# One 64x64 inverse product of the RWKV-7 scan, issued in slot 10 of the group before instead of slot 0 of its own

## The reference

```
def _wkv7_step(S, inp):
    r_t, w_t, k_t, v_t, aa_t, bb_t = inp
    sa = jnp.einsum('zbhij,zbhj->zbhi', S, aa_t)
    S = S * w_t[..., None, :] + sa[..., :, None] * bb_t[..., None, :] + v_t[..., :, None] * k_t[..., None, :]
    y = jnp.einsum('zbhij,zbhj->zbhi', S, r_t)
    return S, y
...
    seq = tuple(jnp.moveaxis(_flip_bwd(z), 2, 0) for z in (r2, w_h, k_h, v2, aa, bb))
    _, ys = lax.scan(_wkv7_step, S0, seq)
```

## Time and profile before

| | |
|---|---|
| median of three runs | 4420.51 us (4414.08 to 4432.33) |
| the profiled execution | 4417.87 us |
| its span, first to last instruction | 4415.9 us |
| mean granted TensorE clock | 0.970 |
| PE busy | 4071.9 us (92%) |
| DVE / ACT / POOL busy | 2155.6 / 1389.2 / 1301.5 us |
| line 1710 (P), PE | 296.3 us in x6400 records |
| lines 1721 and the last level's 1723 | 228.0 us in x5120, and x1280 |

### The profile page before, as it was taken

How to read it: one execution, slowest core, us unless ns; L and a number is a source line. 1 busy time by engine, 2 the same in 40 slices (tenths; PEclk the granted TensorE clock), 3 DMA queues, 4 the chain that set the end, 5 groups by cost and what they waited for, 6 DMA issues and landing times. The chain is left out here.

```text
span 4415.9 us, 108166 instructions
## 1 busy us (share of the span) xinstructions
PE 4071.9 (92%) x47874; PEld 3463.4 (78%) x47874; DVE 2155.6 (49%) x3514; ACT 1389.2 (31%) x2961; POOL 1301.5 (29%) x901
## 2 busy tenths in 40 slices
PE   5999899999999998899958888888879999999999
PEld 5889567888888887788757777777757888888888
DVE  5662462352352442446657777777743343252441
ACT  3331572211111112234435555555532211111111
POOL 3111233211111112122146556566534211111111
PEclk8999899999999998999979999999989999999999
DMA  4222333212213113122232222222143212313213
GB/s 126 71 80 73 121 104 108 68 37 88 81 38 122 51 45 108 63 77 72 96 101 79 80 69 82 69 80 82 46 166 101 81 39 74 98 39 99 69 37 109
DMA packets 354145, 356.39 MB, mean 81 GB/s; under 512 B 18640, under 2 KB 325072, under 8 KB 351632
## 3 DMA queue, kind: packets, MB, share of 16 engines
q1 hardware_dynamic: 352096, 345.19, 24.5%
q10 hardware_dynamic: 1584, 4.27, 0.3%
HBM read 247.16 MB, written 102.24 MB: 79 GB/s over the span
## 5 line engine op out<-in xcount | busy, mean ns | idle before, releaser
L442 POOL TENSOR_TENSOR mo_wlow<-mo_raw,mo_whigh 128x1024 fp32r<-128x1024 f32 (+1 forms) x148 | 350.5, 2368 | 1671.2 <-ACT mo_whigh L529 1671.2
L509 PE MATMUL f_ps<-fx_hh,mo_whigh 128*128 128x512 f32 (+1 forms) x2112 | 529.8, 359 | 0.0
L509 PE MATMUL f_ps<-fx_hl,mo_whigh 128*128 128x512 f32 (+1 forms) x2112 | 529.0, 358 | 0.0
L509 PE MATMUL f_ps<-fx_hh,mo_wlow 128*128 128x512 f32 (+1 forms) x2112 | 528.8, 358 | 0.0
L529 ACT ACTIVATE mo_whigh<-mo_raw 128x1024 fp32r<-128x1024 f32 (+1 forms) x148 | 152.3, 1029 | 863.7 <-PE f_ps L509 863.7
L509 PEld LDWEIGHTS f_ps<-fx_hl,mo_whigh 128*128 128x128 f32 x2112 | 349.1, 189 | 65.4
L509 PEld LDWEIGHTS f_ps<-fx_hh,mo_wlow 128*128 128x128 f32 x2112 | 349.1, 189 | 65.4
L509 PEld LDWEIGHTS f_ps<-fx_hh,mo_whigh 128*128 128x128 f32 x2112 | 349.2, 189 | 64.9
L594 DVE TENSOR_TENSOR f_xo<-f_ps,f_xo 128x512 f32<-128x512 f32 x168 | 90.8, 596 | 611.9 <-PE f_ps L509 579.9
L509 PE MATMUL f_ps<-mo_oh,mo_whigh 128*128 128x512 f32 (+1 forms) x1440 | 362.9, 360 | 9.9 <-PEq L56 9.9
L509 PE MATMUL f_ps<-mo_ol,mo_whigh 128*128 128x512 f32 (+1 forms) x1440 | 360.6, 359 | 0.0
(11 more groups left out here) (293 smaller groups left out, 8449.5 us busy)
## 6 DMA issues: line engine op xcount, KB each, us to landing
f_xo<-xres SPq DMA_DIRECT2D x64, 640.0 KB, 4.0
xres<-f_xo SPq DMA_DIRECT2D x48, 640.0 KB, 2.9
mo_raw<-in_ffn_w_gate SPq DMA_DIRECT2D x44, 512.0 KB, 3.8
mo_raw<-in_ffn_w_up SPq DMA_DIRECT2D x44, 512.0 KB, 3.7
sc_rk<-rkvl SPq DMA_DIRECT2D x80, 256.0 KB, 3.2
rkvl<-ri_ot SPq DMA_DIRECT2D x28, 640.0 KB
mo_raw<-in_ffn_w_down SPq DMA_DIRECT2D x32, 448.0 KB, 4.5
qkv_raw<-in_na_w_qkv SPq DMA_DIRECT2D x24, 512.0 KB, 5.5
```

The costliest lines, as they stand in the source:

```text
L442: nc.gpsimd.tensor_tensor(wlow[:, m % 2, 0:kt], raw[:, 0:kt], whigh[:, m % 2, 0:kt].bitcast(F32), ALU.subtract).then_inc(cut_lo, 1)
L509: last = nc.tensor.matmul(ps[:, m % 2, n, 0:count], w[:, m % 2, k], x[:, k, t0:t0 + count], start=(k == 0 and w is whigh and x is xh), sto ...
```

## The change

`inverse(G, n)` no longer issues anything in slot 0. In slot 10, where P of level INV would be due, it takes P of level 0 of the next group (Gp = G + 1) and interleaves it with T of z = 1, level 4, of group G, two matmuls of the one and two of the other for each chunk. `p_copy` on ACT follows: its copy moves from slot 0 to slot 10, into the place behind `u_copy` and ahead of `fade_state`. What is computed is unchanged, and so is the number of instructions; DVE, POOL and SP keep their order.

```diff
                 def inverse(G, n):
-                    if not group(G) or n > 2 * INV:
+                    if n == 0 or n > 2 * INV:
                         return
                     k, odd = divmod(n, 2)
                     zp = 1 if odd else 0
                     kt = k if odd else k - 1
-                    does_p, does_t = k < INV, kt >= 0
+                    Gp = G
+                    if k == INV:
+                        Gp, k = G + 1, 0
+                    does_p, does_t = group(Gp), group(G)
                     if does_t:
                         level_t_waits(G, 1 - zp, kt)
                     if does_p:
-                        level_p_waits(G, zp, k)
+                        level_p_waits(Gp, zp, k)
                     for s in range(U):
                         for h in range(2):
                             if does_p:
-                                last_p = level_p(G, zp, k, s, h)
+                                last_p = level_p(Gp, zp, k, s, h)
...
                 def p_copy(G, n):
+                    if n == 0 or n > 2 * INV:
+                        return
                     k, z = divmod(n, 2)
-                    if not group(G) or k >= INV:
+                    if k == INV:
+                        G, k = G + 1, 0
+                    if not group(G):
                         return
                     act.wait_ge(pe_p[z], 5 * G + k + 1)
```

## The result

The changed kernel takes 4438.18 us (median of 5 runs, 4436.96 to 4443.01), the kernel before 4420.51 (4414.08 to 4432.33): a ratio of 1.0044, 95% interval 1.0032 to 1.0055. It is 17.7 us slower, less than the 22 us that were set as the bound for slower, and inside the range of 4408 to 4446. The forecast of 4428 had the sign, and half of the size: it was worked out as 8.7 us.

What follows compares the result with a forecast made beforehand. No engine alone was the bound; who waits for whom was, with gram and POOL pinned to DVE's slot 11. 38 x 0.23 = 8.7 us on 4417.87 gave 4426.6, or 4429.2 beside the median; forecast 4428, range 4408 to 4446.

Steps and rivals of the forecast that it cites:

- P is not free in slot 10: Slot 10 on PE: P and T share two quadrants, so both take 0.93 us, 0.46 more than T alone.
- Nothing is to be had from slot 0: Slot 0: removing P frees 0.46 us of PE, but gram waits for DVE's queries, with 0.13 to 0.21 us slack.
- The rival in which the saving arrives: Slots 10 and 0: P and T run side by side or gram's waits don't hold; up to 17.5 us less, 4403; chance 0.08.
- T's result is late at DVE, and with it queries and gram: Slots 10 to 0: DVE takes T 0.27 us after S starts; gram comes 0.14 or 0.32 us later by group.
- The sign to look for: Slot 0 on PE: gram stands behind an idle gap, released by DVE's line 2010, where there was none.
- X is released by ACT's second copy of turn: Slot 11: turn's copies end at 2867.95, so X starts about 2868.0, later after DVE's state than the 0.05 of now.
- The size: 0.23 a group, 8.7 us: Per group: mean of 0.14 and 0.32 us later gram, over 38 groups, 8.7 us slower.
- the rival of P held by DVE: Slot 10: P waits for DVE's slot 9 update and holds T; 0.35 us shift gives 22 us, 4442; chance 0.17.
- The copy of P ahead of the fades: ACT, slot 10: P's copy delays the fades, making DVE's state product wait no more than 0.05 us.
- The half and half of the two kinds of group: Half the groups have gram 0.14 us later, half 0.32; all of one kind gives 5.3 us, of the other 12.2.
- Back to back on one quadrant: Slot 10 rival: successive matmuls on one quadrant don't overlap, 0.22 us a record; 67 us slower, 4487; chance 0.03.
- No change: Scan rival: PE waits without a releaser end at fixed times and swallow a 0.2 us lateness; 4420; chance 0.22.

Runs made afterwards that it cites:

- The other quadrants: Changed kernel with P of slot 10 written to the other PSUM half, so P and T use four quadrants: 1.0047; with ACT's copy also behind the turn copies: 1.0013.
- the kernel with the bare gap: Changed kernel with ACT's copy of P in slot 10 moved behind the two turn copies, PE unchanged: 4442.48 us, ratio 1.0035.
- the two kernels in which T goes first: Changed kernel with slot 10 issuing T whole, then P: 1.0011 with ACT's copy of P behind the turn copies, 1.0060 with it ahead of the fades.
- the kernel with 3200 more instructions: Kernel before with 20 extra 64x64 matmuls per group in slot 10 on free quadrants, result read by nobody: 4468.73 us, ratio 1.0092.

## Why the prediction was right, and where its size was off

*P is not free in slot 10.* Right: 0.93 from the first of P and T to S, as predicted, with lines 1710 and 1723 alternating. The other quadrants give 0.54.

*Nothing is to be had from slot 0.* Right but for a little, and shown by itself: P cut away there gives 0.9997, at most 5.3 us of 15.6. The rival in which the saving arrives falls with it.

*T's result is late at DVE, and with it queries and gram.* Right: the gap of DVE ahead of its slot 10 update is there (31.1 us in 49 waits, 13.6 in 22 before). Predicted 0.27 after S, measured 0.22 in the group shown. The gap of PE ahead of gram that was to show it is not in the changed kernel: X came so late by ACT that its matmuls reach to gram. It is there as soon as ACT's copy is out of the way. The wait was real all the same: gram starts 0.06 behind the queries in the median, and 0.32 behind X, where it follows after 0.28 in the groups in which X itself is late (2.4 and more after S). In the kernel with the bare gap the 0.06 is the same and the 0.32 is 0.60. The forecast of gram at S + 2.29 (2868.32 - 2866.03) stands against a median of 2.33. The sign to look for was badly chosen.

*X is released by ACT's second copy of turn.* Right as to the releaser. That the time came out to the hundredth in the group shown is luck: forecast at about S + 1.97 (2868.0 against S at 2866.03), measured 2950.22 - 2948.25 = 1.97, with a median of 2.01. The copies were forecast to end at S + 1.92 and X to follow at once; they end at S + 1.71 (2949.96 - 2948.25), and X starts 0.26 behind them, in this group and in most. The prediction had no term for the time from ACT's end to PE's start, and it had ACT's block too late by about as much.

*The size: 0.23 a group, 8.7 us.* This is the term that was mis-sized; 17.7 us is 0.47 a group. By the profiles:

```
                                       predicted   measured (two pairs)
slot 10, from P beside T                  +0.46    +0.64  +0.58
slots 11 and 0, given back                -0.23    -0.15  -0.20
slots 1 to 9                               0       +0.10  +0.10
group                                     +0.23    +0.59  +0.48
```

- Slot 10 is 0.12 to 0.18 above the charge of P. In means over 38 groups the first inverse product of slot 10 starts 1.33 after U, against 1.23 before (1.32 and 1.25 in the later pair), and from it to S it is 1.07 against 0.54 (1.06 and 0.55): 0.53 and 0.51 more, not 0.46, the excess being gaps without a releaser. The later start is mostly the rival of P held by DVE: in 6 groups of the one profile and 8 of the other P starts 0.21 or 0.22 behind the end of DVE's slot 9 update, some 0.34 later than usual, which makes 0.05 to 0.07 a group. In the clearest of these

```profile
2797.97 0.28 DVE L2100 TENSOR_TENSOR sc_rf<-sc_inv_ps,sc_rf 128x128 f32<-128x128 f32 x1
```
```profile
2798.01 0.28 PE L1692 MATMUL sc_gram_ps<-sc_small,sc_vb 64*64 64x64 f32 x4
2798.47 0.33 PE L1710 MATMUL sc_inv_ps<-sc_tf,sc_bl 64*64 64x64 f32 x4 [0.18 <-issue]
...
2799.34 0.27 PE L1723 MATMUL sc_inv_ps<-sc_rf,sc_pt_last 64*64 64x64 f32 x1 [0.41 <-issue]
```

  DVE's update of slot 9 ends at 2798.25 and P starts 0.22 later, though the profile writes "issue" in front of it: a wait that was put down to nobody. That it is this wait shows in the two kernels in which T goes first: there, as in the kernel before, the first product of slot 10, which is T's, starts up to 0.13 and 0.21 ahead of the end of that update in such groups, and none is held. The same slot has a second gap, 0.41 in the middle of T, in which no semaphore is waited for. The rival was right in kind, in 6 to 8 of 38 groups and not in all.
- The copy of P ahead of the fades. The prediction gave it "no more than 0.05 of wait". In 31 of 36 groups, the one shown among them, state starts 0.13 after the fades' end, neither more nor less, and 0.85 to 0.89 after DVE took T, where in the kernel before that is 0.81. So the fades do set the start of state in nearly every group, by some 0.05: what was said. Here too two things cancelled, fades that end at S + 0.95 in the group shown and not at S + 1.12 (2867.15 - 2866.03), and 0.13 from ACT's end to DVE's start that the prediction left out. What was wrong was to price the copy alone. Put behind turn's copies it gives back little in the changed order (1.0044 and 1.0038 against 1.0035), but 1.0047 - 1.0013 = 15 us with free quadrants, of which the profiles show 8, and 21.7 us with T first. The prediction counted ACT's copy as a small addition to DVE's lateness; it is a second wait of about the same length beside it.
- The half and half of the two kinds of group was right: 19 groups of the kernel before have gram 0.12 or 0.13 behind the queries, 14 have it 0.18 to 0.22 behind. In medians slots 11 and 0 give back what was forecast: S to the next U is 3.28 before and 3.05 after.
- With the two pairs of profiles as far apart as they are, the split of the 0.24 (0.47 less 0.23) among these is not settled. What is shown is that the copy behind turn's copies, together with either free quadrants or T ahead of P, leaves 5 or 6 us of the loss (1.0011 and 1.0013).

*Back to back on one quadrant.* The rival with 67 us is out: 32 records on two quadrants take 0.93, 58 ns for each on its quadrant.

*No change.* The rival said that fixed gaps would swallow a lateness of 0.2. They did not: the gaps without a releaser are as long as before (118.3 and 123.0 us after, 115.4 and 123.3 before, from 2300 to 3220 us), and the loss came on top.

*What stays open.* The last 5 us in the kernels without both waits: 8 extra matmuls a group on free quadrants also cost 4.9 us, but P is not extra, it is moved, so that the number of instructions is the same. That both are 5 us need not be one cause. A change of order or of number also moves the instructions against the 16,384-byte packets of the next section but one, and no run moves them alone.

## What to carry to other kernels

Before you move work out of a slot, cut it away there and time that: here the answer, 0.9997, would have said that the best outcome is about no change. When a product is put beside another one, count three things apart: the part of the array that both use, the semaphores that the second one waits for on behalf of the first, and the copy that follows it on the next engine, with all that stands behind that copy. And when two such waits are about equally long, each edit alone looks worthless; try them in pairs before you drop either.

## What the runs showed of the hardware

The gaps of PE that nothing releases are not spread at random. In 37 groups of the kernel before, the trace has 219 packets of 16,384 bytes on the queue of kind "instruction", 5.92 for a group, and the 119 such gaps of over 0.15 us (115.4 us) end 1.39 us after the landing of one of them in the median (80% between 1.25 and 1.51, all between 1.20 and 1.64; with a packet every 4 us, gaps at chance times would fall into so narrow a band one time in nine). In the kernel with 3200 more instructions all 139 gaps end 1.20 to 1.64 us after a landing too. Not every packet has a gap. Its row over 2300 to 3220 us (packets, MB, share of 16 DMA engines):

```profile
q8 instruction: 229, 3.75, 1.6%
```

There are 58,457 records of PE in 40 groups, 247 for a packet, so that one is used up in some 4 us (23.76 / 5.92), and 13% of the stretch are such gaps (115.4 of 920). The Trainium skill, Runtime: NRT & Kernel Launch, section Instruction fetch mechanics, says that a boundary of 16 KiB costs one bump of the DMA tail, "mostly hidden". In this trace it is not, if the packets are the cause; for that there are the coincidence in time and the 39 us of the kernel with 3200 more instructions, and no proof.

Matmuls on free quadrants were not free: 4.9 us (0.9 to 8.9) for 1280 instructions more, 39 for 3200.

From the end of an operation to the start of the one on another engine that waited for it alone, the changed kernel shows three distances that repeat over its groups: 0.13 us from ACT's fades to DVE's state (31 of 36), 0.25 to 0.27 from ACT's copy of turn to X on PE (27 of 36), and 0.06 from DVE's queries to gram on PE (the median). The prediction had 0.07 for the last and nothing for the first two.
